# Hybrid encoder layer on one core: attention steps moved later in the work order, first weights asked for on another queue

## What is computed

```python
h = rmsnorm(x, g_mix)
qa, ka, va, qb, kb, vb, ga, gb = split(h @ w_in)
ya = axial_gqa(qa, ka, va, q_gain, k_gain) @ w_a_out      # 8 query heads, 2 key heads
yb = dilated_attention(qb, kb, vb) @ w_b_out              # 3 groups x 4 heads, windows 128/512/2048
x = x + (sigmoid(ga) * ya + sigmoid(gb) * yb) @ w_out
h = rmsnorm(x, g_mlp)
x = x + square(relu(h @ w_up)) @ w_down
return rmsnorm(x, g_final)
```

## Time and profile before

| | us |
|---|---|
| runs of the kernel before, median of 3 (range) | 1168.37 (1167.49 to 1169.94) |
| the profiled execution | 1169.91 |
| its span, first to last instruction | 1168.1 |
| TensorE busy in the span | 1137.3 (97%) |
| VectorE, ScalarE, GpSimd busy | 527.5, 378.5, 321.9 |

### The profile page before, as it was taken

One profiled execution on the slowest core, in us unless ns is written; L12 is line 12 of the kernel. 1 busy time (PEld: TensorE's weight loads), 2 busy tenths in 40 slices (PEclk: granted clock), 3 DMA queues, 4 the chain that ended last, 5 costly groups with the idle time before them and its releaser, 6 DMA issues.

```text
span 1168.1 us, 16275 instructions
## 1 busy us (share of the span) xinstructions
PE 1137.3 (97%) x6210; PEld 1017.4 (87%) x6210; DVE 527.5 (45%) x944; ACT 378.5 (32%) x824; POOL 321.9 (28%) x244
## 2 busy tenths in 40 slices
PE   7898999999999999999999999999999999999997
PEld 6676788888989999999789989898998989898996
DVE  6366544455543445125336526253443526344354
ACT  6424555545555312123134302122130212212122
POOL 5221102020203324044332513324150323324120
PEclk9899999999999999999999999999999999999999
DMA  9402020202001212022422210122222101222202
GB/s 321 138 2 71 1 73 1 74 1 72 2 20 55 76 38 91 3 88 73 181 72 73 72 55 34 57 72 72 72 72 72 58 28 58 72 72 72 72 0 108
DMA packets 47252, 77.13 MB, mean 66 GB/s; under 512 B 7777, under 2 KB 18401, under 8 KB 47201
## 3 DMA queue, kind: packets, MB, share of 16 engines
q1 hardware_dynamic: 43472, 71.83, 18.5%
q10 hardware_dynamic: 3728, 4.61, 1.1%
HBM read 73.20 MB, written 3.22 MB: 65 GB/s over the span
## 4 chain that ended last, share of the span: by engine, by line
PE 93%; DVE 3%; issue 2%; ACT 1%; DMA 0%; ACTq 0%; DVEq 0%
PE unit_ps L732 19%; PE unit_ps L733 18%; PE unit_ps L734 18%; PE score_ps L734 8%; PE score_ps L732 8%; PE score_ps L733 8%; PE turn_ps L851 3%; PE out_ps L881 2%; PE out_ps L869 2%; PE score_ps L812 2%; PE score_ps L838 1%; PE turn_ps L790 1%; PE score_ps L790 1%; PE out_ps L790 1%; PE turn_ps L976 1%
## 5 line engine op out<-in xcount | busy, mean ns | idle before, releaser
L707 POOL TENSOR_TENSOR ring_lo<-ring_whole,ring_hi 128x512 fp32r<-128x512 f32 x236 | 313.2, 1348 | 808.1 <-ACT ring_hi L1010 807.8
L732 PE MATMUL score_ps<-act_hi,ring_hi 128*128 128x384 f32 x512 | 171.4, 335 | 0.0
L734 PE MATMUL score_ps<-act_hi,ring_lo 128*128 128x384 f32 x512 | 171.2, 334 | 0.0
L733 PE MATMUL score_ps<-act_lo,ring_hi 128*128 128x384 f32 x512 | 171.1, 334 | 0.0
L1010 ACT ACTIVATE ring_hi<-ring_whole 128x512 fp32r<-128x512 f32 x236 | 143.6, 626 | 49.5 <-DMA ring_whole<-in_w_up 26.6
L1020 ACT ACTIVATE relu<-score_ps 128x384 f32<-128x384 f32 x64 | 31.5, 493 | 375.6 <-PE score_ps L734 375.6
L734 PE MATMUL unit_ps<-ring_hi,u_lo 128*128 128x512 f32 x384 | 151.5, 395 | 0.0
L732 PE MATMUL unit_ps<-ring_hi,u_hi 128*128 128x512 f32 x384 | 151.5, 395 | 0.0
L733 PE MATMUL unit_ps<-ring_lo,u_hi 128*128 128x512 f32 x384 | 151.4, 394 | 0.0
L732 PE MATMUL unit_ps<-ring_hi,act_hi 128*128 128x512 f32 x336 | 145.4, 433 | 1.2 <-DVE mix_part L1548 1.2
L1391 DVE TENSOR_TENSOR x<-x,unit_ps 128x512 f32<-128x512 f32 x96 | 66.0, 688 | 175.7 <-PE unit_ps L734 175.7
(11 more groups left out here) (188 smaller groups left out, 1662.1 us busy)
## 6 DMA issues: line engine op xcount, KB each, us to landing
ring_whole<-in_w_up SPq DMA_DIRECT2D x64, 256.0 KB, 4.9
ring_whole<-in_w_down SPq DMA_DIRECT2D x64, 256.0 KB, 4.7
ring_whole<-in_w_in SPq DMA_DIRECT2D x48, 256.0 KB, 4.7
ring_whole<-in_w_in SPq DMA_DIRECT2D x62, 128.0 KB, 2.8
ring_whole<-in_w_out SPq DMA_DIRECT2D x16, 256.0 KB, 3.8
xT<-in_x_turned SPq DMA_DIRECT2D x16, 192.0 KB, 4.3
x_in<-in_x_prompt SPq DMA_DIRECT2D x4, 512.0 KB, 7.6
ring_whole<-in_w_a_out SPq DMA_DIRECT2D x16, 128.0 KB, 3.0
```

What stands on the lines that cost most here:

```text
L707: pool.tensor_tensor(ring_lo[:, slot, :], ring_whole[:, slot, :], ring_hi[:, slot, :].bitcast(F32), ALU.subtract).then_inc(lo_cut, 1)
L732: pe.matmul(out, sta[0], mov[0], start=first, stop=False)
L733: pe.matmul(out, sta[0], mov[1], start=False, stop=False)
L734: return pe.matmul(out, sta[1], mov[0], start=False, stop=last)
```

## The change

Four edits, all in the order of work. No instruction of a computation is added or removed.

- **Divisions.** `divide` i and i+1 stand at the end of the even tick i, behind the pair's softmax and the tick's `pv`; before, `divide` i was the first step of tick i+1.
- **Key turns.** `take_keys` turns once more than three tiles wait, instead of two.
- **Attention start.** In the first unit, `qk0` 0, the calls between its parts are `prepare` (which only issues `turn_q` 0) and nothing; tick 0 stands behind the unit. So every tick comes two later. The two empty ticks in `qk2` are gone, and from unit `ga0` 0 on the two lists of steps are the same.
- **Chunk 0.** Its two DMAs are issued first on SyncE's queue, and no longer by ScalarE.

```diff
--- before.py
+++ after.py
@@ -191,8 +191,6 @@
                 units.append(new)
                 if new[0] != "A":
                     units.append(next_unit())
-            if 0 <= i - 1 < len(units) and units[i - 1][0] == "A":
-                steps.append(("divide", i - 1))
             paired = i < len(units) and i % 2 == 0
             early = paired and i and units[i - 1][0] != "A"
             if early:
@@ -205,6 +203,8 @@
                 steps.extend([("softmax", i), ("softmax", i + 1)])
             if 0 <= i - 3 < len(units):
                 steps.append(("pv", i - 3))
+            if paired and units[i][0] == "A":
+                steps.extend([("divide", i), ("divide", i + 1)])
             state["tick"] += 1
 
     waiting = []
@@ -214,9 +214,9 @@
         steps.append(("turn_qk", b, t))
         fresh.append([(b, t), 0])
 
-    def rotated_unit(name, t, rate=0):
-
-        unit(name, t, TILES, rate)
+    def rotated_unit(name, t, rate=0, between=None):
+
+        unit(name, t, TILES, rate, between=between)
         waiting.append((name, t))
         while len(waiting) > 2:
             turn_next()
@@ -240,7 +240,7 @@
             t = keys_left.pop(0)
             steps.append(("take_kva", t))
             waiting.append(("kva", t))
-        if len(waiting) > 2 or (waiting and not keys_left):
+        if len(waiting) > 3 or (waiting and not keys_left):
             turn_next()
         attend(1)
 
@@ -254,6 +254,7 @@
     assert not waiting
     steps.append(("scale_q",))
     state["scaled"] = True
+    attend_late = iter((prepare, lambda: None))
     for name, rate in (("qk0", 3), ("v12", 3), ("qk1", 3), ("qk2", 3)):
         for t in range(TILES):
             if name == "v12":
@@ -261,7 +262,7 @@
                 if waiting:
                     turn_next()
             else:
-                rotated_unit(name, t, rate)
+                rotated_unit(name, t, rate, (lambda: next(attend_late, attend)()) if (name, t) == ("qk0", 0) else None)
             attend(1)
 
     while band:
@@ -663,6 +664,7 @@
                     sp.dma_start(xT[piece(k, half)], x_turned[k, :, half * HALF:(half + 1) * HALF])\
                       .then_inc(xT_landed[k][half], 16)
 
+            load_chunks([0])
             load_xT(0)
             for k in range(1, KC):
                 load_xT(k)
@@ -997,9 +999,6 @@
         @block.scalar
         def _(act):
             act.dma_start(g_col[:, :], g_turned).then_inc(gain_in, 16)
-            for matrix, row, col, width, at, part, rows in plan.chunks[0]:
-                act.dma_start(ring_whole[part:part + rows, 0, at:at + width],
-                              matrices[matrix][row:row + rows, col:col + width]).then_inc(landed[0], 16)
             act.wait_ge(dve_step, 1)
             class_at = [u for u, (branch, _, _) in enumerate(units) if branch in "12"]
```

## The result

| | before | after |
|---|---|---|
| runs side by side, median of 4 (range), us | 1167.93 (1167.07 to 1169.94) | 1154.98 (1154.88 to 1155.31) |
| the profiled execution | 1169.91 | 1155.07 |
| its span | 1168.1 | 1153.3 |
| TensorE busy, idle in the span | 1137.3, 30.8 | 1131.7, 21.6 |

The ratio of the runs is 0.9885, with a 95% interval of 0.9872 to 0.9898: 12.95 us less by the medians, 14.8 by the two spans. The time lies in the range; the forecast of 1152.8 was 2.2 us too low.

The account below looks back on a forecast made before the run. TensorE, busy 97% of the span, bounds the kernel, so only its idle time and clock matter; 5.0 + 4.8 + 3.0 + 1.1 + 1.7 = 15.6 us off the 1168.37 median gives 1152.8, range 1150.5 to 1160.3.

Parts of the forecast that it names:

- Key turns, 5.0: First key turn: 2.05 us of the 3.98 us `tok` wait filled, clock stays up for 2.9 more; 5.0 us, low end 3.3.
- The rival that the clock falls all the same: First key turn: the clock still falls, as 1.93 us idle lies between 1.4 and 3.45; 1154.5 us, chance 0.15.
- Attention later, 4.8: First scores: the 3.45 us wait and 1.7 of low clock go, a new 0.3 wait at `turn_p` comes; 4.8 us.
- Divisions, 3.0: At `turn_p`: four waits for VectorE's divisions go, as both divisions stand before the rotation; 3.0 us, ends 2.0 and 3.2.
- its lower end of 2.0: Divisions at `turn_p`: 2.0 us won if one of the four waits is only exchanged for another.
- Turns in a row, 1.1: Three turns meeting behind unit `qk0` 5: the 1.5 us `qkT` wait shrinks to 0.4; 1.1 us, ends 0.3 and 1.5.
- Chunk 0, 1.7: Kernel start: `xT` lands 2.5 us after issue, so TensorE starts at 5.5 instead of 7.19; 1.7 us, upper end 2.9.
- the 4.5 of the rival: Kernel start: the first `xT` lands 4.5 us after its issue, so chunk 0 wins nothing; 1154.8 us, chance 0.2.
- The loss that the prediction had worked out: Kernel start: no bandwidth won and 0.9 us of SyncE's issue put ahead of `xT`; the sum would be 13.0.
- Half given back later: From 100 us on: TensorE arrives earlier and hidden waits for ScalarE's cuts or VectorE come up; 1160.6 us, chance 0.1.
- slower: VectorE's 0.78 us wait for the second exponential reaches TensorE in each of 20 pairs; 1171.4 us, chance 0.03.
- no change: Waits move but the end is set by weights arriving by time; 1168.4 us, chance 0.02.

## Why the prediction was right, and what was off

**Key turns, 5.0: right in its waits.** `tok` fell by 2.1, as 9 x 0.23 had it, and `k_lo` stayed at 1.4. That the clock holds after 1.93 us was right for the profiled execution and wrong as a rule: it held in the profiled executions of the changed kernel, twice, and in those with the divisions or chunk 0 put back, and fell in those with attention put back and in both with cuts held back. For the sum it mattered little: the two executions of the changed kernel with a mean clock of 0.997 took 1155.31 and 1155.73, the six with 0.999 from 1154.88 to 1155.44. Undoing the edit cost 4.2. The prediction also took the 5.8 and 3.7 us of the earlier trace rows as a sign that the slow stretch varies from run to run; these are two stretches of one execution, and it is the 3.4 us of the run with the key turns put back, behind the same wait of 3.98, that shows the variation. The rival that the clock falls all the same was right in part of the executions, and its own argument, that the second wait hides much of it, is why those runs aren't much slower.

**Attention later, 4.8: the waits were right, but the term hangs on the divisions.** The 3.4 us and the slow stretch went; the new wait was 0.9, not 0.3, as the step took VectorE's maximum at 0.92 from start to exponential, and here an operation of 0.16 took 1.22 beside GpSimd. Taken back, it cost 5.2; alone it won 2.5.

**Divisions, 3.0: the size is right only in the kernel before.** Alone they won 3.75; in the changed kernel they are worth 6.2. The prediction priced each edit at the waits of the trace of before and added them up; with attention later, the old place of the divisions would have brought a new wait of 2.0 beside cuts. Attention and divisions alone won 2.5 and 3.75, and together 6.9 to 7.7, where 4.8 + 3.0 = 7.8 had been priced. That the sum came out near all the same is luck in part: the two edits were made together, so the wait that the prediction had not seen never arose. The term also lacks what the waits for `probs` had covered: one of them is exchanged for 0.5 of `qkT`, as its lower end of 2.0 allowed for.

**Turns in a row, 1.1: the term that was off most.** 0.4 were to stay behind unit `qk0` 5, 1.4 did: 0.87 there, where `qkT` stands behind ScalarE's copy of the unit, and 0.52 at 119.11, behind unit `qk0` 3 and two cuts, which the prediction had not looked for. The runs with and without the divisions' edit show that the 0.52 comes from that edit and not from the turns.

**Chunk 0, 1.7: 1.4 in the wait, 1.4 when undone.** The mechanism was right: the chain of the changed kernel begins

```profile
0.74 0.40 SPq L656
...
1.67 2.88 DMA xT<-in_x_turned
```

so `xT` landed 2.88 us after its issue, not 2.5 and not the 4.5 of the rival, and the two halves of chunk 0 in 2.2 and 2.7, where they had taken 3.0 and 4.81. The loss that the prediction had worked out from the page of the Trainium skill DMA: Bandwidth & Descriptors (Issuing engines are not separate DMA queues) did not come: the edit won 1.4 us. That page speaks of which engine issues; the edit also changed how much was asked for ahead of the first `xT` and chunk 0, and the shorter times to landing fit that. No run changed the queue alone.

**Half given back later, slower, no change:** none came. From 260 to 400 us TensorE is busy for 140.00 us as before, and no wait in the changed kernel's list leads back to the second exponential.

**The sum, and its last step.** Of the spans the change won 14.8, with 15.6 forecast: the missing 1.0 of `qkT`, 0.6 of `probs` and 0.3 of the start stand against 1.0 us more of busy time won than the 4.6 of the two slow stretches. From the 1168.37 of the forecast the median won 13.4 (12.95 from the 1167.93 of the four runs beside it). So 0.8 of the 2.2 us that the forecast missed are in the terms, and 1.4 are in the last step: the profiled execution lay 1.5 us above the median, and the forecast took the whole 15.6 off the median too. After the change the profiled execution lies only 0.1 above. The likely cause, argued from the clocks and not traced, is that the execution of before was above its median because of what the change removes. The executions of the kernel before have a mean granted clock of 0.993 to 0.996 (the profiled one 0.994); those of 1169.4 us and more have 0.993 or 0.994, those under 1168.2 have 0.995 or 0.996, and 0.003 of 1168 us is 3.5 us, about the spread of its runs (1166.4 to 1170.2 over all sets). The changed kernel's clock was 0.999 in six of eight executions, and its runs lie within 0.9 us in each set.

## What to carry to other kernels

Price a slow stretch of the clock from several executions, or take it as a range: what the profiled execution loses to it may be more than the median does. Two edits that move work on the same engine past each other are priced together, in the new timeline, by asking for each moved operation what runs beside it there; terms from the old trace need not add up where the edits share a tick, and a wait that goes may have covered another behind it. And when weights are cut on one engine while another does small operations that a chain waits for, put the cuts behind the chain: two such moves and a better key turn won another 3.3 us here.

## What the runs showed of the hardware that was not expected

- **VectorE beside GpSimd.** While GpSimd subtracts 128x512 tiles, VectorE's operations on SBUF stretch, small ones most: an operation on one column takes 1.22 us instead of 0.16, a scaling of 512 columns up to 1.31 instead of 0.49, two of 256 columns 1.89 and 2.73 instead of 0.61. Holding the cuts back by one semaphore brought 1.22 back to 0.16. Not all are hit alike: the maximum over PSUM at 87.68 kept its 0.68 beside the same cuts. Which operations are hit was not tried further.
- **The clock after a wait of 1.9 us** at the first key turn held at the full level in four profiled executions and fell in three, with the same instructions ahead of it. At the wait of 2.0 for `probs` it fell with the divisions put back (2.01) and held with attention alone later (2.00).
- **The slow stretch at the start is not in the column of the granted clock.** The changed kernel's first matmuls from 5.83 to 11.70 us take 0.42 each, the pitch of the low level, while the window reads 1.00 (and before, from 7.19 to 13.5, likewise):

```profile
5.83:11.70 5.87, 5.87 (x14) 4.65 (x15) 4.32 (x6) 4.35 (x8) 3.64 (x3) 1.00 0.98 328
```

So the start has to be read from durations. The slow stretch hardly became shorter with the earlier start: the first 14 matmuls take 5.90 us (5.83 to 11.73) and took 6.14 before (7.19 to 13.33), about one slow matmul less.
